# One core: a two-block layer with the modulation turned in each group, the first tiles made by the scalar engine, and a norm folded into the gating

## What is computed

```python
mod = jax.nn.silu(c) @ ada_w + ada_b                 # c: 1 x 2048, ada_w: 2048 x 6144
shift, scale, gate = jnp.split(mod, 3, axis=-1)
h = rms_norm(x, norm_g) * (1.0 + scale) + shift
proj = h @ w_in                                      # 2048 x 9296
...                                                  # sparse attention: o_a, recurrence: o_r
o_r = rms_norm(o_r, hgrn_norm_g).reshape(bsz, seq, B_WIDTH) * jax.nn.silu(r_g)
mix = jnp.concatenate([o_a, o_r], axis=-1) @ w_out
x = x + gate * mix
```

## Time and profile before

| | us |
|---|---|
| runs | 2118.72, 2118.79, 2120.5 (median 2118.79) |
| profiled execution, device time | 2115.91 |
| its span in the trace | 2114.1 |
| PE busy | 2063.7 (98%) |
| DVE busy | 1301.9 (62%) |
| ACT busy | 918.0 (43%) |
| POOL busy | 383.9 (18%) |

### The profile page before, as it was taken

One profiled execution on the slowest core, in us unless ns is written; L12 is line 12 of the kernel. 1 busy time (PEld: TensorE's weight loads), 2 busy tenths in 40 slices (PEclk: granted clock), 3 DMA queues, 4 the chain that ended last, 5 costly groups with the idle time before them and its releaser, 6 DMA issues.

```text
span 2114.1 us, 23585 instructions
## 1 busy us (share of the span) xinstructions
PE 2063.7 (98%) x9261; PEld 1625.8 (77%) x9261; DVE 1301.9 (62%) x1657; ACT 918.0 (43%) x1204; POOL 383.9 (18%) x588
## 2 busy tenths in 40 slices
PE   6989999899999999999999999999999999999999
PEld 1258787676888888786788888888888888878887
DVE  4767767889566678865775666554454544444443
ACT  1145523454654544343454434454444444433332
POOL 0000001999999950000000000000000000000000
PEclk9999989999999999999999999999999999999999
DMA  9867656555466675544435555555555656555554
GB/s 347 327 224 253 220 189 203 176 176 170 157 197 203 202 235 179 169 150 139 145 130 170 195 189 179 193 184 190 188 188 191 192 187 195 188 174 193 188 196 159
DMA packets 205680, 408.46 MB, mean 193 GB/s; under 512 B 10825, under 2 KB 12161, under 8 KB 204929
## 3 DMA queue, kind: packets, MB, share of 16 engines
q1 hardware_dynamic: 190480, 376.07, 54.0%
q10 hardware_dynamic: 13330, 24.40, 3.5%
q0 software_dynamic: 1760, 6.49, 1.6%
HBM read 404.83 MB, written 2.10 MB: 192 GB/s over the span
## 4 chain that ended last, share of the span: by engine, by line
PE 91%; DVE 5%; DMA 3%; issue 0%; ACT 0%; SPq 0%; DVEq 0%; ACTq 0%
PE ps L428 81%; PE pm L509 6%; DMA raw<-in_ada_w 3%; PE ps L509 2%; DVE raw_lo L406 1%; PE pm L521 1%; PE pm L577 1%; DMA raw<-in_w_in 1%; DVE mod_part L1190 0%; PE pm L890 0%; DVE proj L1293 0%; DVE xtmp L1388 0%; DVE sc_i L1312 0%; DVE proj L1327 0%; PE pm L839 0%
## 5 line engine op out<-in xcount | busy, mean ns | idle before, releaser
L406 DVE TENSOR_TENSOR raw_lo<-raw,w_hi 128x1024 fp32r<-128x1024 f32 (+1 forms) x648 | 798.0, 1235 | 611.6 <-ACT w_hi L397 603.5
L397 ACT ACTIVATE w_hi<-raw 128x1024 fp32r<-128x1024 f32 (+1 forms) x648 | 679.8, 1050 | 826.9 <-PE ps L428 798.7
L428 PE MATMUL ps<-w_hi,h_hi 128*128 128x512 f32 (+1 forms) x2336 | 941.7, 403 | 16.5 <-DVE raw_lo L406 8.7
L428 PE MATMUL ps<-w_hi,h_lo 128*128 128x512 f32 (+1 forms) x2336 | 913.5, 391 | 0.0
L428 PE MATMUL ps<-raw_lo,h_hi 128*128 128x512 f32 (+1 forms) x2336 | 912.2, 390 | 0.0
L428 PEld LDWEIGHTS ps<-w_hi,h_hi 128*128 128x128 f32 x2336 | 443.0, 190 | 120.4 <-DVE raw_lo L406 13.0
L428 PEld LDWEIGHTS ps<-raw_lo,h_hi 128*128 128x128 f32 x2336 | 443.6, 190 | 93.2 <-issue 7.7
L428 PEld LDWEIGHTS ps<-w_hi,h_lo 128*128 128x128 f32 x2336 | 442.8, 190 | 93.8
L2304 POOL TENSOR_TENSOR proj<-proj 128x128 f32<-128x128 f32 x264 | 183.8, 701 | 12.9
L2304 POOL TENSOR_TENSOR proj<-proj,w1T 128x128 f32<-128x128 f32 x165 | 102.3, 628 | 12.0 <-DMA proj<-in_z 4.7
L428 PE MATMUL ps<-w_hi,hid_hi 128*128 128x512 f32 x256 | 100.5, 393 | 2.0 <-DVE raw_lo L406 2.0
(11 more groups left out here) (309 smaller groups left out, 1203.4 us busy)
## 6 DMA issues: line engine op xcount, KB each, us to landing
raw<-in_w_in SPq DMA_DIRECT2D x140, 1024.0 KB, 5.2
raw<-in_w_ffn_gate SPq DMA_DIRECT2D x44, 1024.0 KB, 5.2
raw<-in_w_ffn_up SPq DMA_DIRECT2D x44, 1024.0 KB, 5.2
raw<-in_w_ffn_down SPq DMA_DIRECT2D x44, 1024.0 KB, 5.1
raw<-in_ada_w SPq DMA_DIRECT2D x32, 1024.0 KB, 7.6
raw<-in_w_out SPq DMA_DIRECT2D x32, 1024.0 KB, 5.1
proj<-in_ada_w ACTq DMA_DIRECT2D x16, 1024.0 KB, 5.2
raw<-in_w_br_hyena SPq DMA_DIRECT2D x8, 1024.0 KB, 5.1
```

Of the source, the lines that this page charges most:

```text
L397: nc.scalar.activation(w_hi[:, p % HRING, :, 0:gm.width(j)], raw[:, k % RING, e:e + HT, 0:gm.width(j)], ACT.Copy).then_inc(hi_done, 1)
L406: nc.vector.tensor_tensor(raw_lo[:, k % RING, e:e + HT, 0:gm.width(j)], raw[:, k % RING, e:e + HT, 0:gm.width(j)], w_hi[:, p % HRING, :, 0 ...
L428: mm = nc.tensor.matmul(ps[pair][:, t, 0:gm.width(j)], l[:, tok], r[:, i, 0:gm.width(j)], start=(k == 0 and q == 0), stop=(k == kt - 1 and ...
```

## The change

1. **Modulation.** PE takes one k tile of chunk 3 instead of two, DVE three instead of two (`ADA_PE`); the budget of DVE's side work after each chunk is 2.5 instead of 3.0. The one-column matmuls that turn the row are made in each group for the group before, not 20 at once after group 5; the first three units of `h` (4 transposes each) are turned after groups 4, 5 and 6, not all three after group 5.
2. **First tiles.** ACT computes both `xtmp` and `h_hi` from PSUM, with scale and bias, two instructions for each k tile; DVE only subtracts. `before_products`, columns and the four first `raw_lo` stay where they are on DVE.
3. **Recurrence's norm.** The 16 multiplications at L1293 are gone. `gate_recurrence(n)` becomes 8 instructions of 128x128 that multiply by `ho` and by the gate. The norm's weights come in as one more row of `rows_b` (one more small load at the start, and PE waits for 11 such loads, not 10), and are applied as a scale in the tiles of `mix` for the recurrence's half: ACT and DVE take two instructions of 256 for a unit instead of one of 512.
4. **Gate rows' sums.** The four matmuls come after parts 82 to 85, in a generator of their own, and DVE's copies at 85 to 88.

```diff
-ROWS_TURNED = 5
+ROWS_TURNED = 4
+ADA_PE = 1
...
-ROWS_B = (("hy_conv_b_2", 24), ("hy_bias_2", 8), ("ada_b", 2 * KT))
-C_NORM, C_MIX, C_FFN, C_CW, C_CB, C_HB, C_AB = 0, KT, 2 * KT, 3 * KT, P, P + 24, P + 32
+ROWS_B = (("hy_conv_b_2", 24), ("hy_bias_2", 8), ("ada_b", 2 * KT), ("hgrn_norm_g", 1))
...
+GATE_SUM_AT = 82
...
-            pe.wait_ge(sig("rows_in"), 16 * 10)
+            pe.wait_ge(sig("rows_in"), 16 * 11)
...
-                    for k in range(CK if c < 3 else HT):
+                    for k in range(CK if c < 3 else ADA_PE):
                         m = mm(ps[g % 2][0:1, 0, :], c_sig[:, CK * c + k:CK * c + k + 1], raw[:, c, k],
                                start=(c == 0 and k == 0), stop=False)
                     m.then_inc(ada_used, 1)
                 pe.wait_ge(mod_parts, 2 * g + 2)
                 mm(ps[g % 2][0:1, 0, :], ones[:, 0:1], mod_part[:, g % 2], start=False, stop=True).then_inc(sig("mod_sum"), 1)
-                if g == ROWS_TURNED:
+                if g >= 1:
+                    pe.wait_ge(sig("mod_read"), g + 2)
+                    for j in range(4 * (g - 1), 4 * g):
+                        mm(mod_bank[:, j:j + 1], mod_row[0:1, j * P:j * P + P], ones[0:1, 0:1])
+                if g >= ROWS_TURNED and g < ROWS_TURNED + 3:
                     pe.wait_ge(sig("h1_rows"), 1)
-                    turn_h1 = turning([("h1", hbuf, KT)])
-                    b = mod_bank
-                if g >= ROWS_TURNED:
-                    pe.wait_ge(sig("mod_read"), g + 2)
-                    for j in range(0 if g == ROWS_TURNED else 4 * (g - 1), 4 * g):
-                        mm(b[:, j:j + 1], mod_row[0:1, j * P:j * P + P], ones[0:1, 0:1])
+                    turn_unit("h1", hbuf, g - ROWS_TURNED)
...
-                pe.wait_ge(gate_used, RING * ADA_GATE + 2)
+
+            def gate_rows():
                 for j in range(ADA_GATE):
-                    yield INDEX_AT[2] + IDX_H // 2 + j
+                    yield GATE_SUM_AT + j
+                    pe.wait_ge(gate_used, RING * ADA_GATE + 2)
                     mm(bank(pe, ("gate", j), "v")[:, :], ones[:], gate[:, j * GW:j * GW + GW]).then_inc(filled, 1)
...
+            def low_of_first(u):
+
+                content(dve, ("h1", u), "v")
+                dve.wait_ge(sig("tile_hi"), u + 1)
+                for k in (2 * u, 2 * u + 1):
+                    i = v.tensor_tensor(h_lo[:, k], xtmp[:, k % 4], h_hi[:, k].bitcast(F32), ALU.subtract)
+                i.then_inc(used["v"], 1)
...
-                    early.step(g, 3.0)
+                    early.step(g, 2.5)
...
-            first_group(g_in, halves_of("h1", KT, 0, lambda k: g_col[:, k:k + 1], lambda k: mod_cols[:, k:k + 1]))
-            drained(("h1", KT // 2 - 1))
+            dve.sem_inc(sig("mod_ready"), 1)
+            for n in range(HRING):
+                low(dve, g_in, 0, n)
+            for u in range(KT // 2):
+                low_of_first(u)
+                if 2 <= u < 2 + g_in.parts - HRING:
+                    low(dve, g_in, 0, u + HRING - 2)
...
-                dve.wait_ge(sig("gains_in"), 64)
-                for t in range(TT):
-                    for h in range(NH):
-                        o = heads(proj, R_Q)[:, t, h]
-                        i = v.scalar_tensor_tensor(o, o, ho[:, t, h:h + 1], gains[:, 3], ALU.mult, ALU.mult)
-                        i.then_inc(v_chain, 1)
-                        links[0] += 1
-                        if h % 4 == 3:
-                            yield OUT_AT + LEAD + 4 + 2 * t + h // 4
-                dve.wait_ge(v_chain, links[0])
...
-                    yield INDEX_AT[2] + IDX_H // 2 + 2 + j // 2 + LEAD
+                    yield GATE_SUM_AT + j + LEAD
                     v.tensor_copy(gate[:, j * GW:j * GW + GW], content(dve, ("gate", j), "v")[:, :]).then_inc(used["v"], 1)
-                    yield 0.7
...
-                o = proj[:, :, R_Q + n * GW:R_Q + n * GW + GW]
-                v.tensor_tensor(o, o, proj[:, :, R_G + n * GW:R_G + n * GW + GW], ALU.mult).then_inc(sig("mix_r"), 1)
+                for t in range(TT):
+                    for h in range(4 * n, 4 * n + 4):
+                        o = heads(proj, R_Q)[:, t, h]
+                        i = v.scalar_tensor_tensor(o, o, ho[:, t, h:h + 1], heads(proj, R_G)[:, t, h], ALU.mult, ALU.mult)
+                        i.then_inc(v_chain, 1)
+                        links[0] += 1
+                dve.wait_ge(v_chain, links[0])
+                dve.sem_inc(sig("mix_r"), 1)
...
-                for p in tile_lows("mix", later(MIX_PARTS)):
+                for p in tile_lows("mix", later(MIX_PARTS), 0, lambda k: cols[:, C_HG:C_HG + 1] if k >= NH else None):
...
+            def tile_of_first(u):
+
+                b = content(act, ("h1", u))
+                if u >= 2:
+                    act.wait_ge(used["v"], units[("h1", u - 2)][2])
+                for k in (2 * u, 2 * u + 1):
+                    src = b[:, (k % 2) * SEQ:(k % 2) * SEQ + SEQ]
+                    for o in (xtmp[:, k % 4], h_hi[:, k]):
+                        i = s.activation(o, src, ACT.Identity, bias=mod_cols[:, k:k + 1], scale=g_col[:, k:k + 1])
+                i.then_inc(sig("tile_hi"), 1)
```

More of the change, by code:

```diff
@@ L851, in attend_second @@
                     turn_unit("ya", q2T, u)
-            class Three:
-                def __init__(self, *works):
-                    self.works = works
-                def step(self, part):
-                    for w in self.works:
-                        w.step(part)
-            chains = Three(beside, Spare(filter_spectrum()), Spare(hyena()), Spare(attend_second()))
+            assert gate_sum.over
+            chains = Chains(mixer, Spare(filter_spectrum()), Spare(hyena()), Spare(attend_second()))
             for j in range(g_i2.groups):
@@ L871, in _ @@
             assert all(w.over for w in chains.works[:3])
-            beside = Three(chains.works[3], Spare(block_two()))
+            beside = Chains(chains.works[3], Spare(block_two()))
             def branch_made(n):
@@ L1026, in row_scale @@
                 dve.wait_ge(sig(name + "_scale"), 1)
-            turned, low_steps, tiles = [0], [0], [0]
-            def first_group(gm, *work):
-                for n in range(HRING):
-                    low(dve, gm, 0, n)
-                n = HRING - 3
-                for w in work:
-                    for _ in w:
-                        if HRING <= n < gm.parts:
-                            low(dve, gm, 0, n)
-                        n += 1
+            tiles = [KT // 2]
             behind = (g_i2, g_b, g_o2, g_f)
@@ L1454, in _ @@
             chain, gate_work, head_work = Spare(block_one()), Spare(gate_row()), Spare(queries_and_keys())
-            beside = ((chain, 1e9), (gate_work, 1.0), (head_work, 1.2))
+            gate_sum = Spare(gate_sums())
+            beside = ((chain, 1e9), (gate_sum, 1e9), (gate_work, 1.0), (head_work, 1.2))
             groups(g_in, range(1, g_in.groups), None, beside)
-            assert gate_work.over and head_work.over
+            assert gate_work.over and head_work.over and gate_sum.over
             def residual(gm, name, gated):
@@ L1907, in _ @@
                     s.activation(lb, lb, ACT.Exp).then_inc(sig("lb_exp"), 1)
-            first_group(g_in)
+            for n in range(HRING):
+                high(act, g_in, 0, n)
+            act.wait_ge(sig("mod_ready"), 1)
+            for u in range(KT // 2):
+                tile_of_first(u)
+                if 2 <= u < 2 + g_in.parts - HRING:
+                    high(act, g_in, 0, u + HRING - 2)
             for q, name in enumerate(("q_norm_g", "k_norm_g", "idx_k_norm_g", "hgrn_norm_g")):
@@ L2057, in block_one @@
                 yield from attend_beside()
-                yield from tile_highs("mix", later(MIX_PARTS))
+                yield from tile_highs("mix", later(MIX_PARTS), 0, lambda k: cols[:, C_HG:C_HG + 1] if k >= NH else None)
                 yield from tile_highs("h2", later(H2_PARTS), 0, lambda k: cols[:, C_MIX + k:C_MIX + k + 1])
```

82 lines of the change are left out of this document (20 added, 62 removed).

## The result

| | before | after |
|---|---|---|
| median of the runs, us | 2118.79 (7 runs, 2113.36 to 2120.5) | 2100.67 (7 runs, 2098.73 to 2109.99) |
| profiled execution, us | 2115.91 | 2106.29 |
| its span, us | 2114.1 | 2104.5 |

The changed kernel takes 0.9922 of the time before, 95% interval 0.9909 to 0.9936: 16.5 us less (2118.79 x 0.0078), between 13.6 and 19.3; the two medians are 18.1 apart. The forecast was 14.4 less, 2104.4 us.

What follows compares the result with a forecast made beforehand. PE, busy 98% of the span, was taken to bound the kernel. Terms -5.0 + 0.8 + 0.3 - 1.7 - 7.2 - 3.7 + 2.1 = -14.4 us took the median from 2118.79 to 2104.4, range 2100 to 2108.5.

Steps and rivals of the forecast that it cites:

- The likeliest case: Whole kernel: the forecast median of 2104.4 us, range 2100 to 2108.5, given 50%.
- The modulation, -5.0 + 0.8 + 0.3 = -3.9: Modulation: last chunk starts 5.0 us earlier, DVE's third k tile costs 0.8, the extra row's load 0.3.
- no large holes: Modulation's transfers: the hole at 92 to 100 us closes, leaving small ones of about 2 us in all.
- the rival's condition: Modulation keeps its pace (13%): DVE's sum 2 us late each group reopens the hole; first term -1, total 2108.4.
- 0.7 us of slack: Modulation: a group costs PE 10.1 us against 10.8 of transfers; only this slack was said to be needed.
- First tiles, -1.7: Before PE's first product part: only DVE's subtraction follows the last load, 1.7 us saved, between 1.0 and 1.8.
- The norm, -7.2: Parts 78 to 81: without DVE's 16 multiplications PE waits less for `raw_lo`, 7.2 us saved, between 4.2 and 7.6.
- The sums of the gate, -3.7: Turned queries: PE no longer waits for gate copies behind the top-k, 3.7 us saved, between 2.0 and 5.9.
- The gating, +2.1: Recurrence's gating: eight DVE instructions replace one, so PE waits 2.1 us more, between 0.9 and 2.7.
- its lower bound: Gating: +0.9 us, if each of the eight instructions takes 0.35 us.
- The sum: Whole kernel: all terms added, -14.4 us.
- Slower, by one-column matmuls in each group: Modulation rival (5%): one-column matmuls drop PE's clock in each group, 28 us over seven groups, total 2137 us.

Runs made afterwards that it cites:

- r_again: The changed kernel once more, unaltered, traced a second time: 2101.73 us, 0.9918 of the kernel before.
- m_pe2: Changed kernel, but PE keeps two k tiles of the modulation's last chunk and DVE two: 0.9917 of the kernel before.
- f_old: Changed kernel with the first tiles as before (DVE scales and shifts, ACT rounds, DVE subtracts): 0.9932 of the kernel before.
- m_old: Changed kernel with the whole modulation stage as before the change: 2109.59 us, 0.9947 of the kernel before.
- best: Changed kernel, PE keeping two k tiles, second gating half a part earlier in two sets, DVE asking POOL two parts later: 2102.88 us, 0.9911 of the kernel before.

## Why the prediction came out as it did

The likeliest case happened, 2100.67 us against 2104.4, inside its range of 2100 to 2108.5. Some of the closeness is luck: of the seven runs four have 2098.7 to 2100.7 and three 2106.3 to 2110.0, so that one run decides on which side the median falls. In the profiled execution the span fell by 9.6 us, in r_again by 16.8, and errors of both signs stand in the sum. Step by step:

- **The modulation, -5.0 + 0.8 + 0.3 = -3.9.** Its end came at 114.4 in the mean of seven traces, 118.6 of the two with the old stage: -4.2. In the single trace of after it is 117.4 to 115.2, only -2.3. The size was right for the mean, the step "no large holes" wasn't: the rival's condition, that DVE's sum comes late, held in seven of eight groups (up to 1.84 us), at a price of some 2 us and not of 4. The statement that 0.7 us of slack is all that is needed was about PE's work and left out DVE's: with seven k tiles and side work it was busy 29.7 of the 31 us between 65 and 96, against 28.3 in m_pe2, which has no such wait. Of the +0.3 for the extra row, 0.0 to 0.4 us is seen: PE's first matmul starts at 10.81 to 11.15 in the thirteen other traces, 10.78 before.
- **First tiles, -1.7.** 7.12 to 5.43, and f_old has 7.12 again. ACT's instructions with two operands by the column took 0.54 us, one started each 0.45 us; DVE stayed last.
- **The norm, -7.2.** -7.34 by parts 77 to 81. The remaining waits were 1.65, 0.18 and 1.12 us, forecast 2.1, 0.4 and 1.3.
- **The sums of the gate, -3.7.** -3.3 in both traces, and 3.6 longer when undone.
- **The gating, +2.1.** The eight took 3.82 us in after and 3.98 in r_again (3.8 forecast), and the wait was 2.0 to 2.4 in seven traces. The mis-sized term is what comes after a wait: in all +2.6 in r_again, +4.1 in after. In four of the seven traces with this wait (after, m_old, m_pe2, f_old) part 154 took 4.4 to 4.8 us instead of 3.2, in the seven without it always 3.2. The working took the wait as its whole price, though it had charged a clock loss to other waits. It also read 0.5 us of slack and took off 0.4, and its lower bound, 8 x 0.35 - 1.48 + 0.2 - 0.4, is +1.1 and not +0.9. By the formula for a float32 tensor_tensor on the page VectorE: DVE Perf Modes of the Trainium skill, section on the TRN2 errata, the eight are an estimated 2.3 us; measured were 3.82, beside POOL.
- **The sum.** Two things that it didn't have: POOL's chain took back 1.5 us in r_again, and the clock in parts 250 to 256 happened to stay up there, 3.2 us. Without these r_again is -16.8 + 3.2 - 1.5 = -15.1, the sum said -14.4. The execution in after had neither; there the start gave -5.0, the norm -7.3 and the sums -3.3, the gating cost 4.1, and parts 50 to 77 took 1.9 more, mostly the clock in the 80-column group, which the sum had at nothing.
- **Slower, by one-column matmuls in each group.** It did not happen: m_pe2 has them in seven groups with a clock of 1.00 at 86 to 100 us and rows at full rate (8.74 us for 20 records). In m_old, with 20 at once, they took 5.92 us and the next 20 records 10.74. That four of them, standing behind a wait for DVE's sum, have a part in the falls of after and r_again isn't excluded. TensorE: Matmul & The Clock Gate of the Trainium skill (section on what is actually happening) ties the clock to how busy PE has been. In this case's traces the 32 records of one column have no idle time around them, and the clock was down behind them in nine traces of twelve: idle time as the profile counts it doesn't explain that fall.

## What to carry to other kernels

Compare two traces by the start of the same piece of work, not by totals: a ledger of stretches finds 0.3 us in 2100. When work is moved from the engine that is bound to one that has a lower share, read that engine's pauses in the very stretch: DVE was busy 62% of the span and 29.7 of 31 us there. Before adding up gains, look for the other engines' long chains that start in the middle and are asked for later: gains between the two beyond the chain's slack turn into a wait. And price a wait of 2 us on TensorE as the wait plus a chance of a slow stretch behind it: behind the gating's wait it came in four traces of seven and cost 1.2 to 1.6 us.

## What the runs showed of the hardware

- One kernel, unaltered, differs by 7.2 us between two executions (0.34%), nearly all at the same few places: behind PE's waits of 1.8 and 2.2 us, in the 80-column group (parts 50 to 58: 30.4 us in eight traces, 31.9 in four, 33.5 in two), at the wait for POOL, and in and after a block of one-column matmuls (24.8, 26.4 or 28.0 us). Behind the gating's wait, in the 80-column group and after the block the loss comes in steps of 1.2 to 1.6 us. The parts between repeat to 0.3 us.
- Small instructions of DVE with both operands in SBUF took 0.48 us for 128x128 while POOL worked, those with one operand in PSUM 0.35. The single instructions of the first kind ran from 0.375 to 0.616 us in after, and from 0.350 in best, so the quickest are as quick as with PSUM; POOL was at work beside all of them. How much of the rest is POOL's doing wasn't tried.
